# Two reordered attention stages in a transformer kernel: index scores and selection of the top-k attention, first linear-attention levels

## The reference, cut to what is computed

```python
dots = einsum('bqhe,bke->bqhk', qib, k_idx)            # 8 index heads
score = einsum('bqh,bqhk->bqk', wb, relu(dots))
score = where(mask, score, -inf)                       # key_chunk <= q_chunk, chunks of 64
vals, idx = lax.top_k(score, topk)                     # topk = 128
kg, vg = gather(k, idx), gather(v, idx)
p = softmax(where(valid, einsum(qb, kg), -inf))
```

## Time and profile before

| | us |
|---|---|
| median of 3 runs | 2516.66 (2512.3 to 2519.39) |
| profiled execution | 2514.6 |
| its span, first to last instruction | 2512.5 |
| mean granted clock of TensorE | 0.962 |
| share of the chain of waits that is work of DVE | 11% |

### The profile page before, as it was taken

The page is one execution under the profiler, slowest core; times in us unless marked ns, Lnnn a source line. Parts: engine busy times, 40 slices in busy tenths (PEclk is TensorE's granted clock), DMA queues, the critical chain, the costliest instruction groups (busy, mean ns, idle before and its releaser), DMA issues.

```text
span 2512.5 us, 28641 instructions
## 1 busy us (share of the span) xinstructions
PE 2353.4 (94%) x11655; PEld 1887.7 (75%) x11659; DVE 1282.0 (51%) x1541; ACT 778.0 (31%) x1003; POOL 137.9 (5%) x92
## 2 busy tenths in 40 slices
PE   6999999996799999999987999999988678999998
PEld 5888888865688888787874788888767446788887
DVE  5434445637544345475467454445556764534443
ACT  3312233233333322353236322122333244322211
POOL 1000001102110100020000100000100000000000
PEclk9999999977899999999999999999999679999999
DMA  4333223210033232233320222332231200323231
GB/s 137 100 101 100 84 83 94 84 55 1 26 101 100 84 100 84 84 100 101 101 68 1 67 95 89 100 100 84 80 95 47 72 1 18 101 88 106 91 100 67
DMA packets 192321, 200.54 MB, mean 80 GB/s; under 512 B 6178, under 2 KB 187520, under 8 KB 192226
## 3 DMA queue, kind: packets, MB, share of 16 engines
q1 hardware_dynamic: 192226, 199.22, 25.1%
HBM read 191.93 MB, written 2.10 MB: 77 GB/s over the span
## 4 chain that ended last, share of the span: by engine, by line
PE 82%; DVE 11%; ACT 3%; issue 2%; DMA 1%; SPq 0%; POOL 0%; DVEq 0%; ACTq 0%
PE psum L548 81%; DVE w_lo L264 1%; DVE sm L1893 1%; PE psum L942 1%; DVE sm L1964 1%; ACT free_h L1100 1%; ACT w_hi L256 1%; PE psum L760 0%; DVE sq L1966 0%; DVE free_h L1473 0%; DVE h_lo L1469 0%; DVE rstd L1484 0%; DVE xg_lo L1466 0%; DVE free_h L1469 0%; DVE free_x L1466 0%
## 5 line engine op out<-in xcount | busy, mean ns | idle before, releaser
L548 PE MATMUL psum<-xg_lo,w_hi 128*128 128x512 f32 x1568 | 610.2, 392 | 5.0 <-DVE xg_lo L1466 2.7
L548 PE MATMUL psum<-xg_hi,w_hi 128*128 128x512 f32 x1520 | 596.3, 392 | 2.7 <-DVE w_lo L264 2.6
L548 PE MATMUL psum<-xg_hi,w_lo 128*128 128x512 f32 x1520 | 593.1, 390 | 0.0
L256 ACT ACTIVATE w_hi<-w_raw 128x2048 fp32r<-128x2048 f32 (+1 forms) x183 | 348.2, 1903 | 530.1 <-PE psum L548 515.2
L264 DVE TENSOR_TENSOR w_lo<-w_raw,w_hi 128x2048 fp32r<-128x2048 f32 (+1 forms) x183 | 419.1, 2290 | 177.3 <-ACT w_hi L256 177.2
L548 PE MATMUL psum<-h_hi,w_hi 128*128 128x512 f32 x1144 | 452.0, 395 | 4.5 <-DVE w_lo L264 2.7
L548 PE MATMUL psum<-h_hi,w_lo 128*128 128x512 f32 x1144 | 446.5, 390 | 0.0
L548 PE MATMUL psum<-h_lo,w_hi 128*128 128x512 f32 x1144 | 446.5, 390 | 0.0
L548 PEld LDWEIGHTS psum<-xg_lo,w_hi 128*128 128x128 f32 x1568 | 296.0, 189 | 68.5 <-issue 4.8
L548 PEld LDWEIGHTS psum<-xg_hi,w_hi 128*128 128x128 f32 x1520 | 286.8, 189 | 66.6 <-issue 5.7
L548 PEld LDWEIGHTS psum<-xg_hi,w_lo 128*128 128x128 f32 x1520 | 286.5, 188 | 59.9
(11 more groups left out here) (235 smaller groups left out, 2264.6 us busy)
## 6 DMA issues: line engine op xcount, KB each, us to landing
w_raw<-in_mlp_w SPq DMA_DIRECT2D x64, 1024.0 KB, 5.2
w_raw<-in_ffn_w_gate SPq DMA_DIRECT2D x22, 1024.0 KB, 5.3
w_raw<-in_ffn_w_up SPq DMA_DIRECT2D x22, 1024.0 KB, 5.3
w_raw<-in_ffn_w_down SPq DMA_DIRECT2D x16, 1024.0 KB, 5.0
w_raw<-in_diff_w_in SPq DMA_DIRECT2D x12, 1024.0 KB, 5.1
w_raw<-in_w_in SPq DMA_DIRECT2D x9, 1024.0 KB, 5.1
w_raw<-in_dsa_w_in SPq DMA_DIRECT2D x9, 1024.0 KB, 5.3
w_raw<-in_ffn_w_down SPq DMA_DIRECT2D x8, 768.0 KB, 4.3
```

Of the source, the lines that this page charges most:

```text
L256: e.activation(w_hi[:, c % 2, 0:n], w_raw[:, c % 2, 0:n], ACT.Copy).then_inc(sem("hi_done"), 1)
L548: return pe.matmul(out, lhsT, rhs, start=start, stop=stop)
```

## The change

**Linear attention.** The level masks are copied ahead of the sliding attention. `gla_diff(0)` and `gla_diff(1)` are done by DVE behind heads 4 and 5, `gla_keys(0)` behind `a1_lo(2)` in head 6, the exps of levels 0 and 1 by ACT at the ends of heads 6 and 7, the memset ahead of `a1_lo(3)`, as soon as the transposes of head 7 are done. The Silus go to the projection before.

**Top-k attention.** The key norm of the index (`kx`) and its turn come one or two steps earlier; `dots(1)` run in steps 2 to 5 of block `c + 5`, `dots(2)` in steps 0 to 3 of `c + 6`, `dots(3)` in tiles 2 to 5 of the query up-projection (`in_uq`), with the ReLUs of block 3 between ACT's copies; the scores of block 3 get a place of their own. Steps of the norms use two banks in turn and come in pairs. The rounds of block 1 are done ahead of the value blocks, those of block 2 within them, and seven of block 3 too; in the attention nine rounds of block 3 are left, one in each of units 0 to 8. The second turn of the queries moves from unit 1 of the attention into the last value block; SP gathers a second half before it scatters a first.

```diff
@@ -294,7 +288,7 @@
...
-        index_score = [None, free_h2[:, 13, :], free_h2[:, 12, :], sq[:, 0, :]]
+        index_score = [None, free_h2[:, 13, :], free_h2[:, 12, :], free_h2[:, 14, :]]
...
@@ -331,8 +325,8 @@
...
-        def spread_bank(name, i):
-            return bank[5] if name in ("sk", "sq") else bank[6 + i % 2]
+        def spread_bank(i):
+            return bank[6 + i % 2]
...
@@ -521,15 +515,14 @@
...
-                if b == 3:
-                    scatter(PACK["sk"], k2, 0)
-                    gather(PACK["sk"] + 1, "sk", k2, 1)
+            gather(PACK["sk"] + 1, "sk", k2, 1)
+            scatter(PACK["sk"], k2, 0)
...
+            gather(PACK["sq"] + 1, "sq", q2, 1)
...
-            gather(PACK["sq"] + 1, "sq", q2, 1)
...
@@ -654,25 +647,23 @@
...
-                if (name, i) in TURNED:
-                    pe.wait_ge(sem("rope_sin"), TURNED[name, i])
-                before = use(name, "_nrm", i if name in ("sk", "sq") else i - 1)
+                if (name, i) == ("sk", 0):
+                    pe.wait_ge(sem("dot_relu"), 24)
+                before = use(name, "_nrm", i - 1)
...
-                dst = spread_bank(name, i)
+                dst = spread_bank(i)
...
@@ -967,8 +958,6 @@
...
                 for u in range(len(units)):
-                    if dsa and u == 1:
-                        rope_turn(PACK["sq"] + 1)
...
@@ -1020,50 +1009,56 @@
...
-                    last = pe.transpose(bank[6][:, n * P:(n + 1) * P], kw[:, n * P:(n + 1) * P], ident[:])
+                    last = pe.transpose(bank[7][:, n * P:(n + 1) * P], kw[:, n * P:(n + 1) * P], ident[:])
...
-                if k == 0:
+                if k == 1:
...
+                if k == 2:
+                    gn_step("kx", 0)
...
-                if k == 4:
-                    pe.wait_ge(sem("widx_read"), 1)
-                    gn_step("kx", 0)
                 if k == 5:
...
-                if k == 7:
+                if k == 6:
                     rope_turn(PACK["kx"])
             def in_k2(k):
+                if k == 1:
+                    gn_stat("sk", 1)
...
-                    gn_stat("sk", 1)
-                if 4 <= k:
-                    dots(1, (2 * k - 8, 2 * k - 7))
+                    pe.wait_ge(sem("widx_read"), 1)
+                if 2 <= k < 6:
+                    dots(1, (2 * k - 4, 2 * k - 3))
...
-                if k == 2:
+                if k < 4:
+                    dots(2, (2 * k, 2 * k + 1))
+                if k == 5:
...
-                if 4 <= k:
-                    dots(2, (2 * k - 8, 2 * k - 7))
+            def in_uq(t):
+                if 2 <= t < 6:
+                    dots(3, (2 * t - 4, 2 * t - 3))
+                if t == 6:
+                    gn_stat("sk", 3)
...
-                if b == 0:
-                    gn_stat("sq", i // 2) if i % 2 else gn_step("sk", i // 2)
-                if b == 1:
-                    dots(3, (i - 1, i)) if i % 2 else gn_step("sk", 4 + i // 2)
-                if b == 1 and i == 5:
-                    rope_turn(PACK["sk"], use("sk", "_nrm", 7))
-                if b == 2 and i in (2, 4, 6):
-                    gn_step("sq", i // 2 - 1)
-                if b == 2 and i == 7:
-                    rope_turn(PACK["sk"] + 1, use("sq", "_nrm", 3))
-                if b == 3 and i in (0, 1, 3, 5, 7):
-                    gn_step("sq", (0, 1, 3, 5, 7).index(i) + 3)
-                if b == 3 and i == 6:
-                    rope_turn(PACK["sq"], use("sq", "_nrm", 7))
+                j = 8 * b + i
+                if j in (2, 4, 6, 8):
+                    gn_step("sk", j - 2)
+                    gn_step("sk", j - 1)
+                if j in (1, 3, 5, 7):
+                    gn_stat("sq", j // 2)
+                if j in (10, 12):
+                    rope_turn(PACK["sk"] + (j - 10) // 2)
+                if j in (14, 16, 18, 20):
+                    gn_step("sq", j - 14)
+                    gn_step("sq", j - 13)
+                if j in (21, 25):
+                    rope_turn(PACK["sq"] + (j - 21) // 4)
...
@@ -1201,10 +1195,14 @@
...
-            def gog_silu(m):
-                act.wait_ge(sem("evac"), c + 9 + m)
-                a(gog[:, 2 * m:2 * m + 2, :], gog[:, 2 * m:2 * m + 2, :], ACT.Silu).then_inc(sem("gog_silu"), 1)
+                if i >= 8:
+                    m = i - 8
+                    act.wait_ge(sem("evac"), c + 9 + m)
+                    a(gog[:, 2 * m:2 * m + 2, :], gog[:, 2 * m:2 * m + 2, :], ACT.Silu).then_inc(sem("gog_silu"), 1)
+            def gla_exp(i):
+                act.wait_ge(sem("gla_d"), i + 1)
+                a(dl[i % 2], dl[i % 2], ACT.Exp, scale=1 / 16).then_inc(sem("gla_e"), 1)
...
@@ -1236,13 +1234,12 @@
...
+                if h >= 6:
+                    gla_exp(h - 6)
...
-            gog_silu(0)
-            gog_silu(1)
-            for i in range(len(LEVELS)):
-                act.wait_ge(sem("gla_d"), i + 1)
-                a(dl[i % 2], dl[i % 2], ACT.Exp, scale=1 / 16).then_inc(sem("gla_e"), 1)
+            for i in range(2, len(LEVELS)):
+                gla_exp(i)
...
@@ -1415,8 +1412,7 @@
...
-            up_copies(c + 3, 4, qi)
-            gn_rms("kx")
+            up_copies(c + 3, 4, qi, between=lambda t: gn_rms("kx") if t == 2 else None)
...
@@ -1430,7 +1426,8 @@
...
-            up_copies(c + 7, KT, q2, 3, between=lambda t: gn_rms("sk") if t == 4 else None)
+            up_copies(c + 7, KT, q2, 3, between=lambda t: relus(3, (2 * t - 6, 2 * t - 5)) if 3 <= t < 7 else None)
+            gn_rms("sk")
...
@@ -1739,21 +1735,6 @@
...
-            a1_max(0)
-            a1_max(1)
-            for h in range(8):
-                a1_norm(h)
-                if h < 6:
-                    a1_max(h + 2)
-                if h % 2 == 0 and h >= 2:
-                    a1_lo(h // 2 - 1)
-            a1_lo(3)
-            link(dve.memset(free_x[:, 0:4, :], 0.0))
-            dve.wait_ge(sem("mix_const"), 32)
-            link(dve.tensor_copy(level[:].rearrange("p a c -> p (a c)"), free_h[:, 12:14, :].rearrange("p a c -> p (a c)")))
...
@@ -1780,16 +1761,33 @@
...
-            gla_diff(0)
+            dve.wait_ge(sem("mix_const"), 32)
+            dve.tensor_copy(level[:].rearrange("p a c -> p (a c)"), free_h[:, 12:14, :].rearrange("p a c -> p (a c)"))
+            a1_max(0)
+            a1_max(1)
+            for h in range(8):
+                a1_norm(h)
+                if h < 6:
+                    a1_max(h + 2)
+                if h % 2 == 0 and h >= 2:
+                    a1_lo(h // 2 - 1)
+                if h in (4, 5):
+                    gla_diff(h - 4)
+                if h == 6:
+                    gla_keys(0)
+            dve.wait_ge(sem("a1_t"), 8)
+            link(dve.memset(free_x[:, 0:4, :], 0.0))
+            a1_lo(3)
...
-            for i in range(nl):
+            for i in range(1, nl):
...
-                if i:
-                    gla_acc(i - 1)
+                gla_acc(i - 1)
...
@@ -1978,64 +1976,64 @@
             gn_split("cq", cq_hi, cq_lo, rsqrt=False)
             evac_scaled(c + 2, kw.unsqueeze(1), ms=(0,))
             lo(dve, c + 4)
-            dve.wait_ge(sem("widx_t"), 1)
-            dve.tensor_scalar(widx, bank[6].rearrange("p (n f) -> p n f", f=P)[:, :, HD:HD + 8],
-                              (8 ** -0.5) * (HD ** -0.5), None, ALU.mult).then_inc(sem("widx_read"), 1)
             gn_rsqrt("kx")
             lo(dve, c + 5)
             gn_scale("kx", 0)
+            dve.wait_ge(sem("widx_t"), 1)
+            dve.tensor_scalar(widx, bank[7].rearrange("p (n f) -> p n f", f=P)[:, :, HD:HD + 8],
+                              (8 ** -0.5) * (HD ** -0.5), None, ALU.mult).then_inc(sem("widx_read"), 1)
             rope(PACK["qi"])
+            rope(PACK["kx"])
             evac_scaled(c + 4, k2[:, 2:4, :])
             lo(dve, c + 6)
-            rope(PACK["kx"])
             index_sum(1)
+            take(1, range(0, 4))
             evac_scaled(c + 5, k2[:, 4:6, :])
             lo(dve, c + 7)
-            take(1, range(0, 4))
             index_sum(2)
+            take(1, range(4, 9))
             evac_scaled(c + 6, k2[:, 6:8, :])
             lo(dve, c + 8)
-            take(1, range(4, 8))
+            take(1, range(9, 11))
+            index_sum(3)
+            take(1, range(11, 16))
+            mask(1)
             gn_rsqrt("sk")
-            take(1, range(8, 12))
             lo(dve, c + 9)
             for i in range(4):
-                gn_scale("sk", i)
-                take(1, range(12 + i, 13 + i))
-            mask(1)
-            lo(dve, c + 10)
-            dve.wait_ge(*use("sq", "_rms", 1))
-            def sk_scale(hh):
-                if hh % 2 == 0:
-                    gn_scale("sk", 4 + hh // 2)
-                if hh == 5:
-                    rope(PACK["sk"])
-            index_sum(3, between=sk_scale)
+                if i == 3:
+                    lo(dve, c + 10)
+                gn_scale("sk", 2 * i)
```

(43 more changed lines are left out.)

19 lines of the change are left out of this document (6 added, 13 removed).

## The result

The changed kernel takes 2502.29 us (median of 7 runs, 2496.58 to 2506.14) where the kernel before takes 2514.29 beside it: a ratio of 0.9942, 95% interval 0.9929 to 0.9955, or 14.6 us less (11.3 to 17.9). The two medians by themselves lie 12.0 us apart; where this text says by how much a kernel is faster, it goes by the ratio. The forecast was 24.5 us less. The measured median lies inside the stated range of 2484 to 2504 us, near its upper end. The profiled execution took 2497.86 us, its span is 2495.9 us, 16.6 less than before, and its mean granted clock 0.966.

What follows compares the result with a forecast made beforehand. PE was busy 94%, so a change pays only where PE waits; DVE bound the first half of the top-k attention. Linear 6.6 plus top-k 17.9 (23.6 - 5.0 - 0.7) made 24.5 us less: 2492.2 us, range 2484 to 2504.

Steps and rivals of the forecast that it cites:

- a first maximum over 10 us late: Top-k attention: a sign that the prediction is wrong; the first maximum itself was forecast 5.0 us later.
- Linear part, 6.6 us: Sliding to linear attention: 9.5 us gained before the first masked add, 2.9 given back; net 6.6, bounds 3 to 8.5.
- PE's empty 10.24 us: Between sliding and linear attention: this empty time of PE was to shrink to under 1 us.
- Attention, 23.6 us: Top-k attention, first maximum to unit 16's: 44.6 us against 68.2, as 20.6 us of rounds leave; 23.6 us gained.
- The pace of the first units: Top-k attention, first units: DVE sets 2.4 to 2.5 us each; PE needs about 2.3 us at the lower clock.
- The full clock before unit 12: First attention stretch: a sign to look for, the granted clock rising above 0.53 before unit 12.
- the clock held low in all units to 15: Rival, top-k attention: units up to 15 at 1.2 GHz, walk ends 8 us later, 2500.2 us; chance 0.17.
- First maximum 5.0 us later: Ahead of the attention: PE reaches first scores 2 us later, DVE's queued rounds and lo(c+13) make the maximum 5.0 later.
- the projections up to the value blocks: Query up-projection: dot products coming in, waits for ReLUs and switches between matmul kinds end the stage 7.5 us later.
- five of their large waits: Value blocks: PE waits of 0.9, 3.1, 3.4, 2.3 and 1.8 us; with small ones 11.9 in all, 2.8 less.
- One extra slow stretch, 0.7 us: Value blocks: one more stretch at the lower clock behind a long PE wait, 1.5 us, partly in DVE's shadow: 0.7.
- DVE as the bound of the value blocks: Rival: PE's steps wait for scales behind DVE's rounds; 2502 us, chance 0.08, or 2512 us, chance 0.04.

Runs made afterwards that it cites:

- experiment 9: The changed kernel with the nine rounds of block 3 moved from units 0 to 8 to units 8 to 16; 0.9951 of the kernel before.
- experiment 3: The changed kernel with unread matmuls of 512 columns filling PE's three waits above 3 us; 0.9952 of the kernel before.
- 5: The changed kernel with the ReLUs of block 3 ahead of ACT's copies in the query up-projection; 0.9902 of the kernel before.
- 12: The changed kernel with five edits: ReLUs first, gn_stat(sk, 1) later, sk's turn and sq's scales earlier, POOL's product after normalisation 7; 0.9854 of the kernel before, 2481.56 us.
- experiment 7: The changed kernel with the first turn of sk ahead of gn_rsqrt(sq) on DVE; 0.9930 of the kernel before.
- 8: The changed kernel with lo(c+12) and lo(c+13) moved from ahead of the first maximum into units 10 and 12; 0.9948 of the kernel before.
- 11: The changed kernel with ReLUs ahead of copies, gn_rsqrt(sk) ahead of rounds, sk's first turn ahead of gn_rsqrt(sq), lo(c+11) behind sq's scales; 0.9906 of the kernel before.
- experiment 10: The changed kernel with gla_keys(0) behind normalisation 7 and not behind normalisation 6; 0.9937 of the kernel before.

## Why the prediction was right in direction and too high in size

The time lies inside the range, but one of the prediction's own signs of being wrong was met: it named a first maximum over 10 us late, and that came 12.1 us late. The range did allow for a late start, but put it down to scales that wait behind DVE's rounds; most of what was late arose in the projections ahead of the value blocks, between PE and ACT. So the median of 2502.29 us meets the 2502 us of that rival by luck. That two misses of the linear part made up for each other was luck. By the prediction's own steps:

- **Linear part, 6.6 us.** Measured 7.3 us at the last masked add, 6.3 with what the products behind it lose (in the 10 us behind that add PE has 0.71 of the clock, before 0.92); 4.3 us (1.5 to 7.0) as a time. Its two terms were both off and made up for each other: the gap behind the last `h_lo` fell by 11.0 us, not 9.5, as the pair matmuls took 2.06 us at the full clock and not 3.8, and the `h_lo` came 3.5 us later (5.2 in the mean of ten executions), not 2.9. The step's reason for the later `h_lo` was wrong. The exp hardly made DVE wait (0.25 us). Behind the keys POOL's product held DVE for 2.1 us. The prediction priced DVE's and POOL's work there as if they did not touch, and yet the price could be read in the trace before, where two differences take 3.42 us beside POOL's product and 1.29 alone (rows in the last section). PE's empty 10.24 us became 1.48, forecast under 1.
- **Attention, 23.6 us.** Measured 23.1: first maximum to unit 16 in 45.2 us, forecast 44.6. The pace of the first units was forecast as 2.4 to 2.5 us, by DVE, and experiment 9 shows that it is DVE. PE was said to need 2.3 us of it at the lower clock; without the rounds a unit takes 1.95.
- **The full clock before unit 12.** Right: windows behind unit 8 have 0.85. With the clock held low in all units to 15, the walk would have been 8 us longer.
- **First maximum 5.0 us later.** This is the step that failed: 12.1 us. Its parts: the projections up to the value blocks were forecast 7.5 us longer, and are 13.2 longer. Of the 5.7 us missing, 4.1 arise ahead of the up-projection, for which the prediction had no term at all: PE's wait for the squares, now 3.66 us and not 2.87, takes the clock down for 2.3 us, and the dots of block 2 wait 1.87 us for a ReLU. 1.6 us are the second ReLU of each pair in the up-projection, 0.48 us for each of three: only the first was counted. The value blocks are 5.1 us shorter, forecast 5.5. All five of their large waits have the forecast size (0.82, 3.25, 3.65, 2.48, 1.66 us, forecast 0.9, 3.1, 3.4, 2.3, 1.8). Slow stretches there cost some 2 us more than in the walk, and something of the same size in it was too long; which term, isn't settled. From the scores to the maximum it is 3.9 us and not 3.0.
- **One extra slow stretch, 0.7 us.** Mis-sized. There are two more than before, and none lies in DVE's shadow. Filling the waits (experiment 3) doesn't bring the time back, taking them out (5 and 12) does, for the most part by the waits themselves.
- **DVE as the bound of the value blocks**, a rival with 0.12, is half true: the waits were of the forecast size, but experiments 7, 8 and 11 show that DVE's queue has no room there, and a wait taken out of it alone comes back at the next scale.
- **Rest.** The 1.5 us less in E are given back behind the last maximum (1.7 us more): executions with 52.8 or 52.9 us in E have 419.7 to 420.0 us behind it, those with 54.4 have 418.2 to 419.2. That is no fixed sum: experiment 7 has 56.0 and 418.8.

In sum, the forecast of 17.9 us for the top-k part against 12.5 - 1.7 = 10.8 us: 6.4 of the 7.1 us missing lie ahead of the first maximum, 0.5 in the attention.

## What to carry to other kernels

When work is put between the tiles of a projection, write down for each inserted piece which engine must answer before the next one, and order that engine's queue so that the answer comes ahead of the wait for the tile's own end: here two lines of ACT's order were worth 9 us. In a full queue, put what another engine waits for (scales, turns) ahead of what nobody waits for (rounds, weights of a later block), and move several of them together; a wait taken out alone comes back one step later. Compare kernels by landmarks inside the stage that changed, with two or three executions of the same kernel beside them.

## What the hardware showed that was not expected

POOL and DVE exclude each other in the products, differences and additions of these traces, which read two operands from SBUF: 1.23 us became 3.40, 0.15 became 2.30, while POOL's product ran 2.35 us; where DVE's keys were under way first (580.16), POOL's took 3.38 us, 1.03 longer. The Trainium skill says this in "SBUF — State Buffer", section "SBUF: two separate sides": the port pair that the two share is an exclusive lock, and whichever starts first has it for the whole instruction. The trace agrees to within 0.15 us: in experiment 10 DVE starts 0.02 us behind POOL and loses 2.17 of the 2.32 us that POOL still has. The masked add, one of whose operands lies in PSUM, shows no sign of it: in the changed kernel it takes 2.46 us (594.64), while POOL's next product runs from 594.75 for 2.37. The kernel before pays the price as well, inside its 13.95 us between the last `h_lo` and the first masked add:

```profile
597.10 3.42 DVE L1466 TENSOR_TENSOR buf_c<-arena 128x512 f32<-128x512 f32 x2 [2.23 <-POOL buf_a L2084]
```

```profile
593.69 3.38 POOL L2084 TENSOR_TENSOR buf_a<-arena,buf_c 128x1024 f32<-128x1024 f32 x1 [102.56 <-ACT buf_c L1100]
597.03 2.34 POOL L2084 TENSOR_TENSOR free_x<-arena,buf_d 128x1024 f32<-128x1024 f32 x1
```

The granted clock also fell where the profile counts PE as busy throughout: in 290 to 300 us, in code that no kernel here changes, PE is busy for 10.00 of 10.00 us, and the clock is 0.86 in experiment 3 (row above) but 1.00 in the changed kernel:

```profile
290.00:300.00 10.00, 10.00 (x44) 7.55 (x43) 5.33 (x9) 4.65 (x4) 0.00 (x0) 1.00 0.25 83
```

"Busy" hides something here. In experiment 3 the fall comes 0.8 us behind eight small matmuls (of one row, one column or 8x8), which take 1.9 us together:

```profile
294.61 1.12 PE L541 MATMUL psum<-arena,mean 1*128 1x512 f32 x2
295.66 0.60 PE L541 MATMUL psum<-sm,arena 128*128 128x1 f32 x4
296.19 0.38 PE L541 MATMUL psum<-sm,mean 8*128 8x8 f32 x2
...
297.32 0.63 PE L541 MATMUL psum<-xg_hi,w_hi 128*128 128x512 f32 x1
```

In the changed kernel the same eight stand at 293.67 and the matmuls behind them keep their 0.39 us. Of the 14 profiled executions of this case eight have this dip, each time within some 1 us behind these eight matmuls, and a second one in 470 to 480 us (0.84 to 0.91), behind a wait of PE of 2.32 us that the changed kernel has as well, without the dip. By the start times of the same code behind them, each costs experiment 3 1.5 us. These eight reach the last projection of the first mixer at 522.6 to 523.5 us. One has only the second (520.5), the five with neither come at 519.0 to 519.6. These 3 to 4 us, and as much again inside the sliding attention, are of the size of the spread between runs of one kernel (9.6 us in the changed one); as only one run of each set was profiled, that they make it up is an inference. No run shows why the same matmuls bring the dip about in one execution and not in another.
